# The opening of a two-layer hybrid diffusion step: smaller first parts, x requested first

## The chip, the cores and the metric

One Trainium2 chip, one of its cores. The metric is the device time of one execution in microseconds (us), median of the runs. One launch computes both layers.

## The reference, cut to what matters

Every layer normalizes x, modulates it with vectors that come from a conditioning vector, and multiplies it by the input projection. The change concerns this beginning in layer 0; attention, output projection and feed-forward follow and are left as they are.

```python
D_MODEL = 2048; SEQ = DEC_SEQ = 128; DEPTH = 2; IN_WIDTH = 4608
def modulation(cond, w_mod, b_mod):            # w_mod: 2048 x 12288
    m = jax.nn.silu(cond) @ w_mod + b_mod
    return jnp.split(m[..., None, :], N_MOD, axis=-1)
...
sm, cm, gm, sf, cf, gf = modulation(c_ctx, mod_w[l], mod_b[l])
h = rms_norm(xp, norm_mix_pre[l]) * (1 + cm) + sm
q_a, k_a, v_a, q_b, k_b, v_b, u_c, v_c = split_projection(h, w_in[l])   # h @ w_in
```

There are two token streams (context and latent, 128 tokens each, called s = 0 and 1), each with its own conditioning vector. All is float32.

## The kernel before, in words

**Products.** A weight piece is 256 rows by 512 columns, 512 KB. SyncE (SP) loads it into a ring of four places (`raw`); ScalarE rounds it into `whi` (fp32r), VectorE writes the rest `raw - whi` into `wlo`, each in rings of four places too. TensorE then does 12 matmuls per piece (`products`, line 956): 2 row blocks of 128, 2 streams, and the three products lo*hi, hi*lo, hi*hi. The activations stand as `xt_hi` and `xt_lo`, transposed, in 16 tiles of 128 rows, k = 0 to 15. `split(q+4)` runs four pieces ahead of TensorE (`LEAD`) and needs the place that piece q gives back when TensorE is done with it (`place_free`, line 529). SP loads raw piece q after `lo_ready` shows piece q-4 split.

**Modulation.** The vectors shift and scale of layer 0 are the first two of six. Each chunk m of 512 columns takes 8 pieces of 512 KB (2 tiles of 128 rows by 512 columns each); `MOD_INIT` = 8 chunks give the two vectors, `start_chunk` puts them in the order 0, 4, 1, 5, 2, 6, 3, 7, so that one chunk of shift and the same chunk of scale come together. A chunk's products go to `bank_M`, ScalarE copies the bank to `mrow` (`row`, line 1297), TensorE turns it by 4 transposes into `bank_T` (`vector_turn`, line 1037), VectorE reduces it into `modt` (`mod_cols`, line 1591). A burst is half a chunk, 4 pieces, put between two pieces of the input projection. Chunks 0 and 1 come ahead of everything; 21 further bursts are at `START_BURSTS`.

**The first unit of layer 0** (`start()`, on TensorE line 966, ScalarE line 1396, VectorE line 1726) is cut into four quarters of `QUARTER` = 18 pieces, q = 0 to 71. Quarter n works with x tiles 4n to 4n+3 only, over all 9 column chunks, two pieces for each chunk. Such a pair of pieces is a visit: it uses banks A0, A1 or B0, B1 in turn, and at its end VectorE reads the banks into z (`read_part`, line 1751; copy in quarter 0, line 1759, and addition later, line 1757). TensorE may begin visit e when visit e-2 is read (`free`). The four engines follow programs written out by hand; VectorE's order for each q is: `split(q+4)`, then the read at a visit's end, then a mod chunk's reduction three pieces after its burst, then the preparation of the next quarter at r = 13 (`part(n+1)`: the vectors, the scaling of two x blocks, the low halves). At r = 12 TensorE has turned the x blocks (`turn_x`).

**The order of the loads.** SP asks for chunk 0 (8 pieces), q = 0, chunk 1 (8), q = 1 to 3, chunk 2 (8), then q = 4, 5, ... with further mod pieces behind loads g+3 and g+4 of a burst at g (`START_FETCH`). Chunks 0 and 1 and half of chunk 2 stand in places of their own; later mod pieces use a ring of four (`mraw`) and wait until the piece four before is used (`mod_room`). GpSimd (POOL) loads 12 constants and then x, one megabyte for each stream. ScalarE does silu of the conditioning, then squares x (8 operations), from which VectorE and GpSimd make the norm. Loads for attention start on POOL when piece `ATT_PIECE` - 1 = 61 of the unit is done.

Of the kernel before, what the change touches and what calls it, by code (L numbers as in the profile page):

```python
# [48 lines left out]
MOD_INIT = 2 * ND  # L49
MOD_WIN = W_INC // 2  # L50
# [101 lines left out]
def ring_piece(m=None, j=0, v=None, i=0):  # L152

    if v is None:
# [15 lines left out]
PE_AT = {ring_piece(m, j): m * UNIT + j for m, j in pe_pieces()}  # L170


N_AT_ONCE = 3 * UNIT


def own_place(q):

    return RING <= q < 2 * UNIT or 2 * UNIT + RING <= q < N_AT_ONCE


def ring_turn(q):

    return q if q < RING else q - (2 * UNIT - RING) if q < 2 * UNIT + RING else q - 2 * UNIT


def ring_before(q):

    n = ring_turn(q) - RING
    return n if n < RING else n + (2 * UNIT - RING) if n < 2 * RING else n + 2 * UNIT
# [32 lines left out]
def mod_tail_of(m):  # L222

    return m if m < MOD_INIT else vector_tail(vector_of(m))


def vector_tail(v):

    return MOD_INIT + v - 2
# [4 lines left out]

def start_piece(q):

    n, r = divmod(q, QUARTER)
    return n, r // 2, 2 * n + r % 2


START_BURSTS = [QUARTER * n + r for n, rs in enumerate(((1, 4, 7, 10, 14), (1, 4, 7, 10, 13, 16), (1, 4, 7, 10, 13, 16), (1, 4, 7, 13)))
                for r in rs]
START_MOD = {g: (2 + i // 2, range(4 * (i % 2), 4 * (i % 2) + 4)) for i, g in enumerate(START_BURSTS)}
START_ENDS = {g: m for g, (m, js) in START_MOD.items() if js[0] and (m < MOD_INIT or m == MOD_INIT + ND - 1)}
ATT_PIECE = QUARTER * 3 + 8
START_FETCH = {g + 3 + h: (m, js[2 * h:2 * h + 2]) for g, (m, js) in START_MOD.items() if m > 2 for h in range(2)}
# [12 lines left out]
class Plan:  # L259
# [3 lines left out]
    def __init__(self):  # L263
# [10 lines left out]
        for l in range(DEPTH):  # L274
# [4 lines left out]
            self.takes(["A0", "A1"], (W_INC + 1) // 2 if l else ND * W_INC // 2)  # L279
            self.takes(["B0", "B1"], W_INC // 2 if l else ND * W_INC // 2)  # L280
# [76 lines left out]
def build_program(nc, a):  # L357
# [8 lines left out]
    with ExitStack() as ctx:  # L366
# [98 lines left out]
        first_landed = [sem(f"first_landed_{i}") for i in range(2 * UNIT)]  # L465
# [84 lines left out]
        def mod_done(l, v):  # L550

            gv = l * 6 + v
            return (gv + 1) * ND if gv < 2 else vector_tail(gv) + 1
# [8 lines left out]
        def mod_place(q):  # L562

            if not own_place(q):
                return mraw[:, q % RING]
            i = q - RING
            if i >= 2 * UNIT:
                hi = spare[:].rearrange("p k t -> p (k t)")
                lo = gate_ffn[:].rearrange("p s d -> p (s d)")
                t = (hi, lo)[i % 2][:, (4 + 4 * (i // 2 % 2)) * 2 * P:][:, 0:KB * CH]  # L570
                return t.rearrange("p (t n) -> p t n", t=KB)
            if i >= 10:
                return (hid, sil)[i - 10][:]
            t = z[:, i // 4, i % 4 * KB * CH + 4 * P:][:, 0:KB * CH] if i < 8 else qkt[:, 8 * (i - 8):8 * (i - 7), :].rearrange(
                "p h c -> p (h c)")
            return t.rearrange("p (t n) -> p t n", t=KB)
# [10 lines left out]
        def mraw_ready(engine, q):  # L587

            if own_place(q):
                engine.wait_ge(first_landed[q - RING if q < 2 * UNIT else q - 2 * RING], 16)  # L590
# [3 lines left out]
        def xt_count(l, which):  # L594


            return 8 + 9 * (2 * l + which)
# [14 lines left out]
        def vec_count(l, which):  # L612

            return 2 * l + which + ND
# [10 lines left out]
        def _(sp):  # L625
            def mod_room(q):

                if q < RING or own_place(q):
# [41 lines left out]
            def mod_chunk(m, l, js=range(UNIT), col=None):  # L670

                for j in js:
                    q = ring_piece(m, j)
                    if m < MOD_INIT:
                        src = a["mod_w"][l, j * KB * P:(j + 1) * KB * P, col * CH:(col + 1) * CH]
                        mod_room(q)
                        sp.dma_start(mod_place(q), src.rearrange("(t p) n -> p t n", p=P)).then_inc(
                            first_landed[q - RING if q < 2 * UNIT else q - 2 * RING] if own_place(q)
                            else mraw_landed[q % RING], 16)
# [28 lines left out]
            for m in range(2):  # L708
                mod_chunk(m, 0, range(UNIT), start_chunk(m))
# [1337 lines left out]
```

## Time and profile before

| | |
|---|---|
| median of 3 runs | 2320.89 us (2319.48 to 2322.94) |
| profiled execution, its time | 2317.93 us |
| its span, first to last instruction | 2316.2 us |
| busy: PE / DVE / ACT | 97% / 70% / 43% of the span |
| granted TensorE clock, mean | 0.996 |
| chain that ended last, share of PE | 87% |
| moved by DMA | 610 MB, 263 GB/s over the span |

PE is TensorE's matmuls, PEld its weight loads, DVE VectorE, ACT ScalarE, SPq the queue of SyncE. Times in rows are us from the span's start unless they say ns; "x24" is the number of instructions merged in a row; what stands in brackets is idle time before it and what ended that. The end of a matmul is modelled, so a short stall between two can be missing.

### The profile page before, as it was taken

What the parts mean: (1) busy time and instruction counts of PE and PEld (TensorE: products, weight loads), DVE (VectorE), ACT (ScalarE), POOL (GpSimd) and SP (SyncE); (2) the same over time, 40 slices, a digit from 0 to 9 for tenths busy, and PEclk for the clock granted to TensorE, in tenths of its full rate; (3) what the DMA queues carried; (4) which work ended last, traced back from release to release, by engine and by line L of the source; (5) the groups of instructions that cost most, each with busy time, mean ns of one, the idle gap of its engine ahead of it and who ended that gap; (6) DMA issues with size and microseconds to landing.
All of it is one profiled execution on the core that took longest, in us unless ns stands there. A gap on an engine that the chain in (4) does not pass through costs nothing.

```text
span 2316.2 us, 27842 instructions
## 1 busy us (share of the span) xinstructions
PE 2247.0 (97%) x10614; PEld 1778.0 (77%) x10614; DVE 1622.3 (70%) x1734; ACT 984.9 (43%) x1277; POOL 66.5 (3%) x97
## 2 busy tenths in 40 slices
PE   5999989999999999999999999999999999999998
PEld 3766666678888888888877886787888888888886
DVE  3555473488988989889887996557888544554555
ACT  3333253464444444334446344346444444434443
POOL 1000120000000000000000101000000000000000
PEclk9999999999999999999999999999999999999999
DMA  9899989868878878888866998766887666666664
GB/s 364 323 334 341 337 317 330 300 220 289 282 271 292 289 265 283 295 279 290 307 209 225 312 315 283 271 204 207 270 263 263 185 196 185 190 189 193 191 225 146
DMA packets 269365, 609.91 MB, mean 263 GB/s; under 512 B 19100, under 2 KB 19280, under 8 KB 267824
## 3 DMA queue, kind: packets, MB, share of 16 engines
q1 hardware_dynamic: 264832, 589.37, 75.4%
q0 software_dynamic: 4400, 18.75, 2.3%
q8 instruction: 85, 1.39, 0.2%
q14 instruction: 48, 0.39, 0.0%
HBM read 603.79 MB, written 5.45 MB: 263 GB/s over the span
## 4 chain that ended last, share of the span: by engine, by line
PE 87%; DVE 4%; DMA 4%; ACT 3%; issue 1%; POOL 1%; SPq 1%; POOLq 0%; DVEq 0%; ACTq 0%
PE bank_A L961 41%; PE bank_B L961 39%; DMA mraw<-in_mod_w 3%; PE bank_X L1049 2%; PE bank_M L1025 2%; DVE wlo L1564 1%; PE bank_M L1009 1%; ACT junk L1285 1%; ACT whi L1271 1%; DMA x<-in_x_sample 0%; DVE x L1674 0%; ACT prob L1436 0%; PE bank_M L950 0%; DVE xt_lo L1615 0%; PE bank_T L1042 0%
## 5 line engine op out<-in xcount | busy, mean ns | idle before, releaser
L1564 DVE TENSOR_TENSOR wlo<-raw,whi 128x1024 fp32r<-128x1024 f32 x724 | 880.6, 1223 | 587.3 <-ACT whi L1271 586.4
L1271 ACT CAST whi<-raw 128x1024 fp32r<-128x1024 f32 x724 | 759.5, 1051 | 1162.6 <-PE bank_A L961 575.5
L961 PE MATMUL bank_B<-whi,xt_lo 128*128 128x512 f32 x1104 | 433.3, 392 | 0.0
L961 PE MATMUL bank_A<-whi,xt_lo 128*128 128x512 f32 x1088 | 428.9, 394 | 3.7 <-DVE xt_lo L1615 3.7
L961 PE MATMUL bank_B<-wlo,xt_hi 128*128 128x512 f32 x1104 | 430.0, 389 | 0.0
L961 PE MATMUL bank_B<-whi,xt_hi 128*128 128x512 f32 x1104 | 429.8, 389 | 0.0
L961 PE MATMUL bank_A<-wlo,xt_hi 128*128 128x512 f32 x1088 | 425.0, 391 | 0.0
L961 PE MATMUL bank_A<-whi,xt_hi 128*128 128x512 f32 x1088 | 424.7, 390 | 0.0
L1585 DVE SCALAR_TENSOR_TENSOR acc<-mraw,cond,acc 128x1024 f32<-128x1024 f32 x300 | 371.2, 1279 | 0.0
L961 PEld LDWEIGHTS bank_A<-whi,xt_lo 128*128 128x128 f32 x1088 | 205.0, 188 | 65.1 <-issue 23.2
L961 PEld LDWEIGHTS bank_B<-whi,xt_lo 128*128 128x128 f32 x1104 | 207.2, 188 | 53.8 <-issue 11.7
L961 PEld LDWEIGHTS bank_B<-whi,xt_hi 128*128 128x128 f32 x1104 | 207.2, 188 | 43.7
L961 PEld LDWEIGHTS bank_B<-wlo,xt_hi 128*128 128x128 f32 x1104 | 207.3, 188 | 42.1
L961 PEld LDWEIGHTS bank_A<-whi,xt_hi 128*128 128x128 f32 x1088 | 204.9, 188 | 43.6
L961 PEld LDWEIGHTS bank_A<-wlo,xt_hi 128*128 128x128 f32 x1088 | 204.9, 188 | 41.6
L961 PE MATMUL bank_A<-whi,ht_lo 128*128 128x512 f32 x352 | 138.3, 393 | 0.7 <-DVE wlo L1564 0.7
L961 PE MATMUL bank_B<-whi,ht_lo 128*128 128x512 f32 x352 | 137.6, 391 | 0.2 <-DVE wlo L1564 0.2
L961 PE MATMUL bank_A<-whi,ht_hi 128*128 128x512 f32 x352 | 137.1, 389 | 0.0
L961 PE MATMUL bank_B<-wlo,ht_hi 128*128 128x512 f32 x352 | 137.0, 389 | 0.0
L961 PE MATMUL bank_A<-wlo,ht_hi 128*128 128x512 f32 x352 | 137.0, 389 | 0.0
L961 PE MATMUL bank_B<-whi,ht_hi 128*128 128x512 f32 x352 | 137.0, 389 | 0.0
L961 PEld LDWEIGHTS bank_A<-whi,ht_lo 128*128 128x128 f32 x352 | 66.1, 188 | 16.7 <-issue 2.3
(242 smaller groups left out, 1567.7 us busy)
## 6 DMA issues: line engine op xcount, KB each, us to landing
mraw<-in_mod_w SPq DMA_DIRECT2D x352, 512.0 KB, 6.0
raw<-in_w_gate SPq DMA_DIRECT2D x176, 512.0 KB, 4.4
raw<-in_w_up SPq DMA_DIRECT2D x176, 512.0 KB, 4.4
raw<-in_w_down SPq DMA_DIRECT2D x176, 512.0 KB, 5.0
raw<-in_w_in SPq DMA_DIRECT2D x144, 512.0 KB, 5.4
raw<-in_w_out SPq DMA_DIRECT2D x64, 512.0 KB, 5.8
z<-in_mod_w SPq DMA_DIRECT2D x12, 512.0 KB, 11.5
spare<-in_mod_w SPq DMA_DIRECT2D x8, 512.0 KB, 9.5
```

The lines of the kernel that those rows point to most:

```text
L961: mm = pe.matmul(bank[f"{pair}{s}"][:], xs[:, k, t], w[:, kb, :], start=(k == first and n == 0), stop=(k == (nk - 1 if last is None else l ...
L1009: mm = pe.matmul(bank["M"][g:g + 32, :], cond[:, 2 * k:2 * k + 32], w[:, kb, :], start=(k < 4), stop=(k >= KD - 4))
L1025: mm = pe.matmul(bank["M"][32 * c:32 * c + 32, :], cond[:, 2 * k:2 * k + 32], w[:, c % 2, :], start=(k == 0), stop=(k == KD - 1))
L1049: mm = pe.transpose(bank[b][:, n * P:(n + 1) * P], t, ident[:])
L1271: act.copy(weights(u * UNIT + ph)[0], raw[:, ph % RING]).then_inc(hi_ready, 1)
L1285: act.activation(junk[:], src, ACT.Square, accum_out=dst).then_inc(sq_ready, 1)
L1564: dve.tensor_tensor(lo, raw[:, ph % RING], hi.bitcast(F32), ALU.subtract).then_inc(lo_ready, 1)
L1585: ins = dve.scalar_tensor_tensor(out=to, in0=w, scalar=c, in1=to, op0=ALU.mult, op1=ALU.add)
```

## The change

- `HALVED` = 2: chunks 0 and 1 are worked as halves of 256 columns. A piece is now 4 tiles of 128 rows by 256 columns (still 512 KB, contiguous rows of 1 KB in place of 2 KB), and four pieces make a complete half. Only the first half of each comes ahead of the projection. The second halves are bursts after q = 1 and q = 4. Their copies, transposes and reductions are done for each half (2 transposes in place of 4).
- The first quarter's x tiles come as two parts of two: `PARTS` is {0,1}, {2,3}, {4..7}, {8..11}, {12..15}. Pieces q = 0 to 8 go over the 9 column chunks with tiles 0 and 1, q = 9 to 17 with tiles 2 and 3. So in the first quarter each piece is a visit of its own, with its own bank pair and its own read into z.
- The scaling and the low halves for tiles 2 and 3 come at q = 7, those for tiles 4 to 7 at q = 16 (before: r = 13).
- Bursts are now after q = 6, 9, 11, 13 in the first quarter (before: 1, 4, 7, 10, 14); quarters two and three keep r = 1, 4, 7, 10, 13, 16; quarter four has 1, 4, 7, 9, 13 (before: 1, 4, 7, 13). In all 21 as before, and the two halves besides.
- SP asks for x first, then first half of chunk 0 (4 pieces), q = 0, first half of chunk 1 (4), q = 1, 2 pieces, q = 2, 2 pieces, q = 3, 4 pieces (the second halves), then q = 4, 5, ...; chunk 2 isn't loaded ahead any more. ScalarE squares x ahead of silu.
- `ATT_PIECE` - 1 goes from piece 61 to piece 63.

```diff
+PARTS = [range(0, 2), range(2, 4), range(4, 8), range(8, 12), range(12, 16)]
+VISITS = 2 * W_INC + (ND - 1) * W_INC
 def start_piece(q):
     n, r = divmod(q, QUARTER)
-    return n, r // 2, 2 * n + r % 2
+    return (r // W_INC, r % W_INC, r // W_INC) if n == 0 else (n + 1, r // 2, 2 * n + r % 2)
...
+    return q if q < QUARTER else QUARTER + (q - QUARTER) // 2
...
+START_HALVES = {1: 0, 4: 1}
+START_BURSTS = [QUARTER * n + r for n, rs in enumerate(((6, 9, 11, 13), (1, 4, 7, 10, 13, 16), (1, 4, 7, 10, 13, 16), (1, 4, 7, 9, 13)))
...
+START_TURNS = {QUARTER * n + 12: n + 1 for n in range(ND - 1)}
+START_SCALES = {7: 1, 16: 2, QUARTER + 13: 3, 2 * QUARTER + 13: 4}
+ATT_PIECE = QUARTER * 3 + 10
...
-            for m in range(2):
-                mod_chunk(m, 0, range(UNIT), start_chunk(m))
-                for q in range(1, LEAD) if m else range(1):
-                    start_load(q)
-            mod_chunk(2, 0, range(UNIT), start_chunk(2))
+            for s in range(2):
+                sp.dma_start(x[:, s, :], xin[s]).then_inc(x_loaded, 16)
+            mod_chunk(0, 0, range(0, 4), start_chunk(0))
+            start_load(0)
+            mod_chunk(1, 0, range(0, 4), start_chunk(1))
+            for q, (m, js) in enumerate(((0, range(4, 6)), (0, range(6, 8)), (1, range(4, 8)))):
+                start_load(q + 1)
+                mod_chunk(m, 0, js, start_chunk(m))
...
             def start():
-                for m in range(2):
-                    mod(m)
-                    mod_tail(m)
+                mod(0, range(0, 4))
+                start_tail(0)
                 turn_x(0, 0, 0)
                 turn_x(0, 0, 1)
+                mod(1, range(0, 4))
+                start_tail(1)
...
+            def halved_piece(m, j):
+
+                q = ring_piece(m, j)
+                w = mod_place(q) if q in OWN else mraw[:, q % RING].rearrange("p t (h n) -> p (t h) n", n=CH // 2)
+                for t in range(4):
+                    k = 4 * (j % 4) + t
+                    mm = pe.matmul(bank["M"][32 * t:32 * t + 32, 0:CH // 2], cond[:, 2 * k:2 * k + 32], w[:, t, :],
+                                   start=(k < 4), stop=(k >= KD - 4))
+                mm.then_inc(mod_used, 1)
...
                 for q in range(ND * QUARTER):
-                    n, c, _ = start_piece(q)
-                    r = q % QUARTER
+                    p, c, _ = start_piece(q)
                     split(0, q + LEAD)
-                    if r % 2:
-                        read_part(n, c, q)
+                    if visit_ends(q):
+                        read_part(p, c, q)
                     if q - 3 in START_ENDS:
-                        m = START_ENDS[q - 3]
-                        mod_cols(m, start_chunk(m))
-                    if n + 1 < ND and r == 13:
-                        part(n + 1)
+                        start_cols(START_ENDS[q - 3])
+                    if q in START_SCALES:
+                        part(START_SCALES[q])
```

## Rows read from the trace of the kernel before

**Rows 1.** The page, the span in 40 slices of 57.9 us.

```profile
GB/s 364 323 334 341 337 317 330 300 220 289 282 271 292 289 265 283 295 279 290 307 209 225 312 315 283 271 204 207 270 263 263 185 196 185 190 189 193 191 225 146
```

**Rows 2.** Stretches: length, busy us (instructions) of five engines, TensorE clock, DMA.

```profile
20.70:38.20 17.50, 8.17 (x49) 3.26 (x49) 6.59 (x19) 9.87 (x23) 0.73 (x1) 0.90 1.05 408
...
38.19:45.45 7.26, 7.26 (x24) 5.53 (x25) 4.99 (x7) 1.77 (x2) 1.18 (x2) 0.76 1.05 405
...
45.30:283.80 238.50, 233.66 (x1182) 161.18 (x1181) 133.56 (x170) 81.91 (x93) 8.77 (x13) 1.00 0.93 333
...
80.00:98.00 18.00, 18.00 (x94) 13.60 (x93) 11.00 (x19) 8.13 (x12) 0.55 (x1) 1.00 0.68 234
```

**Rows 3.** Waits of TensorE, 45 to 285 us: total, times, longest.

```profile
PE bank_M L1025 <- DMA mraw<-in_mod_w: 3.9, 3, 2.6
```

**Rows 4.** Timeline up to the first product: start, us, engine, operation, idle before.

```profile
14.75 0.23 ACT L1467 ACTIVATE silu_c<-vcols 128x32 f32<-128x32 f32 x1 [12.73 <-DVE vcols L1905]
...
15.25 3.58 PE L1009 MATMUL bank_M<-mraw,cond 128*32 128x512 f32 x16 [1.26 <-DVE cond L1907]
...
19.13 0.63 ACT L1285 ACTIVATE junk<-x 128x512 f32<-128x512 f32 x1 [4.14 <-DMA x<-in_x_sample]
...
25.03 0.57 ACT L1300 COPY mrow<-bank_M 128x512 f32<-128x512 f32 x1
...
32.33 0.59 ACT L1300 COPY mrow<-bank_M 128x512 f32<-128x512 f32 x1 [5.79 <-PE bank_M L1009]
...
38.19 0.47 PE L961 MATMUL bank_A<-whi,xt_lo 128*128 128x512 f32 x1 [3.69 <-DVE xt_lo L1615]
```

**Rows 5.** Timeline of ScalarE: piece q = 4 is rounded.

```profile
47.73 1.05 ACT L1271 CAST whi<-raw 128x1024 fp32r<-128x1024 f32 x1 [7.76 <-DMA raw<-in_w_in]
```

**Rows 6.** The chain that ended last, in order of time: pieces and a burst.

```profile
38.19 7.33 PE bank_A L961 x24
...
47.37 5.71 PE bank_B L961 x24
53.08 2.72 PE bank_A L961 x12
55.80 1.85 PE bank_M L1009 x16
```

**Rows 7.** Timeline of VectorE: split of piece 6, read of the second visit.

```profile
54.26 1.23 DVE L1564 TENSOR_TENSOR wlo<-raw,whi 128x1024 fp32r<-128x1024 f32 x1 [0.62 <-ACT whi L1271]
55.40 1.28 DVE L1759 TENSOR_SCALAR z<-bank_B 128x512 f32<-128x512 f32 x2
56.97 1.23 DVE L1564 TENSOR_TENSOR wlo<-raw,whi 128x1024 fp32r<-128x1024 f32 x1 [0.29 <-ACT whi L1271]
```

**Rows 8.** Timeline of VectorE: the preparation of the second quarter.

```profile
92.01 0.18 DVE L1599 TENSOR_REDUCE modt<-bank_T 128x8 f32<-128x32 f32 x1
...
92.71 1.37 DVE L1645 TENSOR_SCALAR xtmp<-bank_X,scal,shift 128x128 f32<-128x128 f32 x4
94.77 1.29 DVE L1615 TENSOR_TENSOR xt_lo<-xtmp,xt_hi 128x512 fp32r<-128x512 f32 x2 [0.69 <-ACT xt_hi L1289]
```

**Rows 9.** Timeline of TensorE: first matmul of the second quarter (q = 18).

```profile
101.34 0.39 PE L961 MATMUL bank_B<-whi,xt_lo 128*128 128x512 f32 x1
```

**Rows 10.** The chain again: mod pieces' landings, and a burst behind one.

```profile
101.48 7.85 DMA mraw<-in_mod_w
...
270.18 11.50 DMA mraw<-in_mod_w
281.81 2.00 PE bank_M L1025 x8
...
285.09 6.97 DMA raw<-in_w_out
```

**Rows 11.** Timeline of GpSimd: the first load for attention.

```profile
259.67 0.87 POOL L784 DMA_DIRECT2D prob<-in_cache_a_k  x1 [162.51 <-PE bank_A L961]
```

**Rows 12.** DMA queues, 262 to 274 us: packets, MB, share of 16 engines.

```profile
q0 software_dynamic: 772, 2.20, 67.7%
```

More of the change, by code:

```diff
@@ L49 @@
 MOD_INIT = 2 * ND
+HALVED = 2
 MOD_WIN = W_INC // 2
@@ L152, in ring_piece @@
 def ring_piece(m=None, j=0, v=None, i=0):
+    if v is None and m < HALVED:
+        return UNIT * (j // 4) + 4 * m + j % 4
     if v is None:
@@ L168, in vector_of @@
     return 0 if m < MOD_INIT else MOD_PE[(m - MOD_INIT) // ND]
[L170 to L178, printed above, removed]
+PE_AT = {ring_piece(m, j): ring_piece(m, j) if m < HALVED else m * UNIT + j for m, j in pe_pieces()}
+OWN = [*range(0, 12), *range(16, 20)]
 def ring_turn(q):
-    return q if q < RING else q - (2 * UNIT - RING) if q < 2 * UNIT + RING else q - 2 * UNIT
+    return q - (12 if q < 16 else 16)
 def ring_before(q):
-    n = ring_turn(q) - RING
-    return n if n < RING else n + (2 * UNIT - RING) if n < 2 * RING else n + 2 * UNIT
+    return q - RING if q >= 24 else q - 2 * RING
 BANKS = ["A0", "A1", "B0", "B1", "M", "X0", "X1", "T"]
@@ L464, in build_program @@
         mraw_landed = [sem(f"mraw_landed_{i}") for i in range(RING)]
-        first_landed = [sem(f"first_landed_{i}") for i in range(2 * UNIT)]
+        first_landed = [sem(f"first_landed_{i}") for i in range(len(OWN))]
+        part_scaled = [sem(f"part_scaled_{s}") for s in range(2)]
         apart_landed = [sem(f"apart_landed_{i}") for i in range(4)]
@@ L594, in xt_count @@
         def xt_count(l, which):
-            return 8 + 9 * (2 * l + which)
+            return 10 + 9 * (2 * l + which)
         def z_complete(engine, l):
@@ L612, in vec_count @@
         def vec_count(l, which):
-            return 2 * l + which + ND
+            return 2 * l + which + len(PARTS)
         N_CONST = 12
@@ L796, in _ @@
             load(edge[:], a["c_edge"], const_loaded)
-            for s in range(2):
-                load(x[:, s, :], xin[s], x_loaded)
             def power(src, dst, s_in, n_in, s_out):
@@ L1040, in vector_turn @@
                 free("T", i)
-                for t in range(4):
+                for t in range(2 if i < 2 * HALVED else 4):
                     mm = pe.transpose(bank["T"][:, t * P:(t + 1) * P], mrow[:, t * P:(t + 1) * P], ident[:])
@@ L1299, in row, with start_row, pre_part @@
                     act.wait_ge(filled["T"], i)
-                act.copy(mrow[:], bank["M"][:]).then_inc(mrow_ready, 1)
+                c = slice(0, CH // 2 if i < 2 * HALVED else CH)
+                act.copy(mrow[:, c], bank["M"][:, c]).then_inc(mrow_ready, 1)
+            def start_row(i):
+                act.wait_ge(mod_used, 4 * (i + 1) if i < 2 * HALVED else
+                            (i - HALVED) * UNIT + UNIT if i - HALVED < MOD_INIT else (MOD_INIT + ND) * UNIT)
+                row(i)
+            def pre_part(p):
+                fill_of(*plan.at[(0, "pre_uses", 0)][1])
+                bk, n = plan.at[(0, "pre_uses", 0)][1]
+                for k in PARTS[p]:
+                    ins = act.activation(xtmp[:, 0, 1, k, :], bank[bk][:, k * P:(k + 1) * P], ACT.Identity,
+                                         scale=scal[:, k, 1:2], bias=shift[:, k, 1:2])
+                ins.then_inc(freed[bk] if p else part_scaled[1], 1)
+                for s in range(2):
+                    bk, n = plan.at[(0, "pre_uses", 0)][s]
+                    if p:
+                        act.wait_ge(freed[bk], n + 2)
+                    else:
+                        act.wait_ge(part_scaled[s], 1)
+                    ks = slice(PARTS[p][0], PARTS[p][-1] + 1)
+                    high(xt_hi[:, ks, s * P:(s + 1) * P], xtmp[:, 0, s, ks])
             def pre_scale(l, which, i):
```

158 lines of the change are left out of this document (94 added, 64 removed).

## The prediction

> **What bounds the kernel now.** I read the slices of the whole span first [rows 1]: DMA moves 300 to 364 GB/s in the first eight slices (463 us) and 146 to 225 in the last eight, so memory can only matter early. The stretches come next [rows 2]. From 20.7 to 38.2 us DMA runs full, 408 GB/s, while TensorE is busy for 8.17 of 17.5 us: there the data decide. From 45.3 to 283.8 us TensorE is busy for 233.66 of 238.5 us, at the full clock, with DMA at 333 GB/s: there TensorE's own program decides, and its waits for data are three, 3.9 us in all [rows 3]. From 80 to 98 us DMA falls to 234 GB/s while TensorE is full: the rings hold the loads back, not memory. So after the opening, whatever makes TensorE idle is lost for good, and a microsecond won at the first product counts only if the products behind it come as early.
>
> The timeline to the first product [rows 4] shows what the change attacks. The constants give silu at 14.75, chunk 0's matmuls go from 15.25, but x lands only at 19.13, its eight squares hold ScalarE to 25.0, and the copy of chunk 0 stands behind them at 25.03. Chunk 1 is complete at 32.33, and the first product starts at 38.19.
>
> **The first product.** Landings follow from bytes, since DMA is full. Piece q = 4 is rounded at 47.73, right after a wait for its data [rows 5]. Ahead of its landing stand 29 pieces with it (8+1+8+3+8+1) of 0.524 MB, x (2.10) and the constants (0.46): 17.8 MB. After the change 21 pieces stand there (4+1+4+1+2+1+2+1+4+1), 13.6 MB in all: 4.19 MB less, at 408 GB/s 10.3 us less. So q = 4 can be rounded at 37.4. The first half of chunk 1 is complete after 7.3 MB, 15.4 us before that, at 22.0. x is first and lands near 10; squares to 16, silu behind them, half of chunk 0 for 3.6 us at the clock of the first burst [rows 4], its copy and turn and the eight turns of x for some 2 us: 22. Then the half of chunk 1, 1.85 [rows 6] to 3.6 us, and what is 5.9 us now (32.33 to 38.19) less 0.9 for x's turns, done already, and about 1.4 for work on two tiles in place of four: 3.6. First product at 27.5 to 29.2, some 9 us sooner.
>
> **The third piece.** Here the gain is cut. Each of the first 18 pieces is now a visit with banks of its own, and TensorE may start visit q only when VectorE has read visit q-2. VectorE's order is split(q+4), then the read of q. The read of q = 0 stands behind the split of q = 4, so behind its landing: 37.4, rounding 1.05, split 1.23 with the read's 1.28 [rows 7] give 40.95. TensorE by then has done q = 0 and 1 and the second half of chunk 0 (7.3 us warm, 9.2 with the slow stretch of 7.33 for 24 matmuls in place of 5.44 [rows 6]): ready at 36 to 38, idle for 3 to 5 us. Now q = 2 starts at 47.37 [rows 6], so it comes 6.4 us sooner. But less mod work is done by then: 20 of 21 bursts are still to come at that point now, and 22 of 23 after the change. Two bursts at 1.85: 3.7 us of the 6.4 are owed.
>
> **The first quarter as a recurrence.** A piece is 2.72 us, a burst 1.85 [rows 6]. From the end of a piece to the end of its read: 53.08 to 56.68, 3.60 us (wait, rounding, split, read) [rows 6, 7]; with the wake-up 3.65. Now that stands beside two further pieces (5.44) and is hidden; after the change one piece (2.72) covers it, and 0.93 us show wherever no burst, turn (0.87) or tail (0.27) stands between. Worked from q = 2 at 40.95: q = 4 waits 0.65 for the read of q = 2. q = 7 ends at 62.2. Behind its read VectorE now prepares tiles 2 and 3. The same for four tiles takes 92.01 to 96.06, 4.05 us [rows 8]; two tiles, by halving the four- and two-instruction groups but not the 0.7 us ahead of them, 2.5. So q = 9 starts at 62.2+3.6+2.5+0.3 = 68.6, where q = 8 was done at 64.9: 3.7 us idle. The burst after 11 comes two pieces behind the burst after 9, whose ring places it needs: its four pieces and a raw piece land about 8 us after the places come free (a mod piece takes 7.85 us to land in such company [rows 10]), so its last piece waits about 1.0. q = 16 waits 0.6. q = 16 ends at 99.0; its read, the 4.05 of the full preparation and 0.35 give 107.0 for q = 18, where q = 17 was done at 101.7: 5.3 us idle. Before, this preparation stood at r = 13, three pieces earlier in the order and thus hidden. Stalls in all 0.65+3.7+1.0+0.6+5.3 = 11.3.
>
> Now q = 18 starts at 101.34 [rows 9]; after, at 107.0. It is 5.7 us late, and one burst more (17 against 16) is still to come: 7.5.
>
> **The rest.** Quarters two and three have the bursts where they were and cost nothing new; their cover is 5.4 us for each read, as now. In the last quarter the burst after 63 is two pieces behind that after 61, again 1.0: 8.5. [...] After the gap before 38.19 the clock is 0.76 in the next 7.26 us [rows 2], 1.9 us lost; after the 2.63 us for the burst at 281.81, eight matmuls take 2.00 in place of 1.07 [rows 10], 0.9 lost. Three new gaps at 0 to 1.9 each: 0 to 5, taken as 1.0, like the nearer row: 3.0. Given back: the burst after 67 now waits 2.6 us [rows 3] for data that take 11.5 us to land beside attention's loads, asked for from 259.67 [rows 10, 11]; these come two pieces later now. It may save 0 to 3.5 (stall and clock); I take 1.5, as output-projection pieces (6.97 us to land [rows 10]) meet those loads instead. Sum 8.5+3.0-1.5 = 10.0 us. Against the profiled execution, 2317.9 (1.7 more than its span), that is 2327.9. The median shown is 3.0 above that execution; on it the forecast is 2331.
>
> **Rows of 1 KB.** No row shows the halved pieces' load (a row of 256 columns is 1 KB in place of 2). The nearest end is that it moves like the 2 KB rows, cost 0. The far end is the software queue with its 256 to 512 byte rows: 2.20 MB in 67.7% of 12 us [rows 12] is 271 GB/s of full engines against 389 (408 at share 1.05). Sixteen such pieces, 8.4 MB, would take 9.4 us more, and q = 2 would come that much later. [...] I take 0, nearer in kind (same queue, double length), and half the far end, 4.7, for the range. The Trainium skill (DMA: Bandwidth & Descriptors, Specifications) gives 512 bytes as the least for line rate, by which this would cost nothing; the trace has no hardware-queue load with rows under 2 KB to test it.
>
> The Trainium skill (TensorE: Matmul & The Clock Gate, HAM oscillation) speaks against the change's gaps: idle stretches between matmul groups drop the clock, and the work behind them runs slow. The slow matmuls behind 38.19 and 281.81 agree; by it the sum would sit at the upper end, 10.0+2.0.
>
> **The rivals.** (1) The first product is what counts, and the rest keeps its pace. For it: TensorE is busy for 98% behind 45 us, and 9 us are won at the front. Then 9.7 less 3.7 for the two bursts moved behind, with 1 to 3 from the burst after 67: about -8, 2313. It needs VectorE's reads not to hold TensorE: that q = 2 not wait for q = 4's landing, which the order split-before-read contradicts. (2) The mechanism is mine but the stalls are short: preparation of two blocks overlaps more than I think, the clock holds, the burst at 67 doesn't wait. 6.4-3.7 = 2.7 lead against 5 to 7 of stalls and no clock loss: 0 to +4, 2321 to 2325. (3) Slow rows of 1 KB, or the clock low through much of the first quarter: +13 to +19, 2334 to 2340. (4) The start is limited by memory all through, so that TensorE's extra idle time only replaces waits for data: against it, DMA at 234 GB/s from 80 to 98 and 3.9 us of data waits in 238; it would give 2320.9. It goes into (2).
>
> **How the numbers follow.** Forecast (+5 to +13, 2326 to 2334) 0.60; (1) 0.10; (2) with (4) 0.18, a little of it below; (3) 0.12. The predicted time is 2331. The range for 8 in 10 runs from 2320 (case 2's lower end, leaving out case 1) to 2338 (case 3's middle and above). A measurement of this kernel can tell 0.2%, 4.6 us, from no change: slower than 2325.5 is the forecast, case 3 and a bit of case 2, 0.72; faster than 2316.3 is case 1, 0.10; within, 0.18.
>
> **What would show it.** In the profile of the changed kernel: the first product between 27 and 30 us; an idle gap of 3 to 5 us before the third piece, released by a VectorE read near 41 that follows a wait of ScalarE for raw data; TensorE waits on the read of the banks of about 0.9 us in the first quarter; gaps of 3 to 4 us before q = 9 and some 5 us before q = 18, each ending on an xt_lo operation; q = 18 near 107 to 111. I'm wrong if q = 2 starts before 36, if q = 18 starts before 101, or if the first quarter shows no waits for VectorE.

## The result and the profile after

The changed kernel takes 2342.60 us (median of 4 runs, 2338.84 to 2343.79), the kernel before 2321.91 (4 runs, 2319.48 to 2323.30): ratio 1.0086, 95% interval 1.0071 to 1.0100, so 20.7 us slower. The profiled execution took 2341.53, its span is 2339.7. The forecast was 2331, in a range up to 2338: the sign was right, the size half of what came, and the time lies outside the range.

The page of the kernel after, DMA rate in 40 slices. The last eight are nearly what they were [rows 1]; the first two are lower, 334 and 269 against 364 and 323.

```profile
GB/s 334 269 310 328 357 323 312 298 207 300 288 265 290 291 262 293 286 283 289 289 243 201 309 333 259 300 192 212 254 278 261 196 192 188 189 189 195 192 220 149
```

**The first product comes 10.9 us sooner.** Timelines of ScalarE and TensorE of the kernel after, up to the first product (start, us, engine, line, operation, idle before):

```profile
8.59 0.63 ACT L1331 ACTIVATE junk<-x 128x512 f32<-128x512 f32 x1 [6.56 <-DMA x<-in_x_sample]
...
14.60 1.28 ACT L1542 ACT_TABLE_LOAD   x1
15.90 0.23 ACT L1542 ACTIVATE silu_c<-vcols 128x32 f32<-128x32 f32 x1
...
16.40 3.40 PE L1055 MATMUL bank_M<-z,cond 128*32 128x256 f32 x32 [2.26 <-DVE cond L1991]
...
21.54 1.93 PE L1055 MATMUL bank_M<-z,cond 128*32 128x256 f32 x32
...
27.34 0.77 PE L989 MATMUL bank_A<-whi,xt_lo 128*128 128x512 f32 x1 [2.93 <-DVE xt_lo L1691]
```

x's squares begin at 8.59, not 19.13; half of chunk 0 goes at 16.40, half of chunk 1 at 21.54, and the first product starts at 27.34, where it was 38.19 [rows 4]. A second table load of 1.28 us has come in ahead of silu, which now stands behind the squares.

**At the third piece half of that is gone.** The chain of waits of the kernel after, in order of time (start, us, what):

```profile
29.34 9.29 DMA raw<-in_w_in
...
38.65 1.05 ACT whi L1317
...
40.87 0.69 DVE z L1843
...
42.25 5.08 PE bank_A L989 x12
```

The landing of raw piece q = 4 (38.6) releases the rounding, the rounding the split, the split lets VectorE come to the read of q = 0 at 40.87, and that read lets q = 2 start at 42.25. TensorE had been idle for 4.62 us, and its next twelve matmuls took 4.91 us instead of 2.72 (counted here and below from start to start; the chain's 5.08 goes to the end of the last one). In the kernel before q = 2 started at 47.37 [rows 6]: the lead is 5.1 us.

**At q = 18 the lead is a lag.** Waits of TensorE of the kernel after, 27 to 118 us (total, times, longest):

```profile
PE bank_A L989 <- DVE xt_lo L1691: 8.0, 2, 5.1
PE bank_A L989 <- DVE z L1843: 5.3, 2, 4.6
PE bank_B L989 <- DVE xt_lo L1691: 3.7, 1, 3.7
...
PE bank_M L1045 <- DMA mraw<-in_mod_w: 0.4, 1, 0.4
```

The 8.0 are 2.93 before the first product and 5.09 before q = 18; the 5.3 are 4.62 before q = 2 and 0.72 before q = 4; the 3.7 stand before q = 9. These three are waits for VectorE, where the kernel before had none from its first product to 285 us. VectorE of the kernel after, timeline of the preparation ahead of q = 18:

```profile
109.78 1.28 DVE L1841 TENSOR_TENSOR z<-z,bank_A 128x512 f32<-128x512 f32 x2
110.97 0.18 DVE L1675 TENSOR_REDUCE modt<-bank_T 128x8 f32<-128x32 f32 x1
...
113.72 1.29 DVE L1691 TENSOR_TENSOR xt_lo<-xtmp,xt_hi 128x512 fp32r<-128x512 f32 x2 [0.68 <-ACT xt_hi L1335]
```

It takes 4.04 us, as before [rows 8], but it now follows the read of q = 16, and q = 18 starts right behind it, at 115.28. Before, q = 18 started at 101.34 [rows 9]: 13.9 us late. (Leads and lags are against one trace of the kernel before, and that trace is a quick one: in the trace of experiment 3, of a kernel with the same opening, the first product starts at 39.60, q = 2 at 48.61 and q = 18 at 103.34.)

Stretches of the kernel after (length, busy us and instructions of TensorE, its weight loads, VectorE, ScalarE, GpSimd, then TensorE's granted clock, DMA share, GB/s):

```profile
42.25:115.28 73.03, 62.63 (x309) 42.93 (x309) 43.98 (x69) 22.07 (x30) 0.53 (x1) 0.94 0.78 274
...
115.28:304.65 189.37, 180.72 (x909) 122.96 (x909) 99.96 (x126) 59.72 (x67) 8.20 (x12) 0.98 0.91 325
...
42.20:47.30 5.10, 5.05 (x13) 4.03 (x14) 2.29 (x3) 0.00 (x0) 0.00 (x0) 0.56 0.81 256
...
72.90:77.50 4.60, 4.55 (x16) 3.19 (x20) 2.42 (x3) 0.25 (x1) 0.53 (x1) 0.63 0.39 127
...
115.20:122.50 7.30, 7.22 (x28) 5.61 (x32) 3.63 (x4) 1.05 (x1) 0.00 (x0) 0.78 0.27 74
```

From q = 2 to q = 18 the kernel after takes 73.0 us, the one before took 54.0. Of the 73.0, 10.4 are idle. Behind each of the three gaps the granted clock is low, 0.56, 0.63 and 0.78 of 2.4 GHz: the twelve matmuls of q = 2 take 4.91 us, those of q = 9 4.46, where 2.72 is the full clock's, and the 24 of q = 18 and 19 take 7.2 where they took 5.6 in the kernel before. That makes 2.2, 1.7 and 1.6, in all 5.5 us.

Two bursts are slow without a long wait in the list. TensorE's timeline of the burst after q = 11:

```profile
85.37 1.93 PE L1045 MATMUL bank_M<-mraw,cond 128*32 128x512 f32 x12
87.67 1.05 PE L1045 MATMUL bank_M<-mraw,cond 128*32 128x512 f32 x4 [0.37 <-DMA mraw<-in_mod_w]
```

It takes 3.28 us, where a burst whose data are there takes 1.85, and the burst after q = 13 takes 2.54. Their weight loads wait for the mod pieces one by one, 2.8 us in four waits between 60 and 115 us.

**The last quarter takes 4.5 us more in two waits.** Waits of TensorE of the kernel after, 118 to 310 us, and the chain of waits there:

```profile
PE bank_M L1071 <- DMA mraw<-in_mod_w: 8.1, 5, 5.9
```

```profile
275.81 7.24 DMA mraw<-in_mod_w
...
283.18 1.13 PE bank_M L1071 x8
...
284.64 17.93 DMA mraw<-in_mod_w
...
302.71 1.94 PE bank_M L1071 x8
304.64 6.38 PE bank_B L989 x24
```

The burst after 63 waits 1.22 us for a landing of 7.24. The one after 67 waits 5.87 for a landing of 17.93 us, where it waited 2.6 for one of 11.50 [rows 3, 10]. The first of attention's twelve loads goes out at 281.55, 3.1 us ahead of that landing's start; before, it was 259.67 [rows 11]. GpSimd's timeline of the kernel after:

```profile
281.55 0.87 POOL L815 DMA_DIRECT2D prob<-in_cache_a_k  x1 [207.78 <-PE bank_A L989]
```

The piece behind that burst starts at 304.57, before at 283.68, a lag of 20.9 us. It stays to attention's first turn of z, 320.16 against 299.31. The spans differ by 23.5, so some 2.6 us come later: TensorE waits 1.6 us for a mod piece near 459 us, and some 1.1 us are added between 1120 and 1510 us, far from the change, where experiment 9's trace loses over 3 us against the same trace of the kernel before. The medians differ by 20.7.

### The profile page after: what moved, and what is told of

Its sections match the earlier page's. It is cut to its first block, busy times and chain, and to the rows that moved or that the text cites. A ratio compares the mean times of both kernels' runs of the same rounds, so it can differ in the third digit from the quotient of the medians.

```text
span 2339.7 us, 28083 instructions
## 1 busy us (share of the span) xinstructions
PE 2255.2 (96%) x10678; PEld 1786.5 (76%) x10678; DVE 1634.3 (70%) x1759; ACT 986.4 (42%) x1282; POOL 65.5 (3%) x95
## 4 chain that ended last, share of the span: by engine, by line
PE 85%; DMA 5%; DVE 5%; ACT 3%; issue 2%; SPq 1%; POOL 0%; POOLq 0%; DVEq 0%; ACTq 0%
PE bank_A L989 40%; PE bank_B L989 38%; DMA mraw<-in_mod_w 4%; PE bank_X L1095 2%; PE bank_M L1071 2%; DVE wlo L1635 1%; PE bank_M L1045 1%; ACT junk L1331 1%; ACT whi L1317 1%; DVE acc L1656 0%; DVE x L1750 0%; SPq L668 0%; ACT prob L1507 0%; DMA raw<-in_w_in 0%; PE bank_M L978 0%
## 5 line engine op out<-in xcount | busy, mean ns | idle before, releaser
L989 PE MATMUL bank_A<-whi,xt_lo 128*128 128x512 f32 x1092 | 433.3, 397 | 13.9 <-DVE xt_lo L1691 8.0
```

What stands on the lines that cost most here:

```text
L989: mm = pe.matmul(bank[f"{pair}{s}"][:], xs[:, k, t], w[:, kb, :], start=(k == first and n == 0), stop=(k == (nk - 1 if last is None else l ...
```

## The experiments

All times are medians; the ratio is to the kernel before on the same chip, with its 95% interval, which is about 3 us to either side; of a difference between two of the kernels below it is about 4. Differences of less than that are carried by the traces, not by the times.

**1. Reads ahead of splits.** The kernel after, in whose first quarter VectorE reads the banks of piece q before it splits q+4:

```diff
                     p, c, _ = start_piece(q)
+                    if q < QUARTER:
+                        read_part(p, c, q)
                     split(0, q + LEAD)
-                    if visit_ends(q):
+                    if q >= QUARTER and visit_ends(q):
                         read_part(p, c, q)
```

> The changed kernel with one thing altered: in the first quarter VectorE reads a piece's banks ahead of the split of the piece four further on. Theory R (what holds the first quarter is the read queued behind the split, 3.6 us after a piece's end against 2.72 of cover): the 4.6 us idle before the third piece goes, the third piece starts near 37.7 in place of 42.25, the waits of 0.5 to 0.9 for reads go, the slow matmuls behind the gap at 42.25 (2.2 us) go in part; the gaps before q = 9 (3.7) and q = 18 (5.1) get shorter by some 1 us at most. But q = 4 can't start before its own split, about 41 to 42, so the win at q = 4 is only what remains: start near 43.2 against 51.02. In all 6 to 9 us less than the changed kernel's 2342.6: 2334 to 2337. Rival M (memory, not the order of reads, holds the first pieces): the idle time moves to the wait for the raw pieces q = 4 and 5 and at most 2 us are won: 2340 to 2343.

Measured: 2334.98 us, ratio 1.0053 (1.0039 to 1.0066), 7.6 less than the kernel after. Waits of TensorE of this kernel, 27 to 110 us:

```profile
PE bank_A L989 <- DVE xt_lo L1691: 6.9, 2, 4.0
PE bank_B L989 <- DVE xt_lo L1691: 2.6, 1, 2.6
PE bank_B L989 <- DVE z L1845: 2.2, 1, 2.2
```

q = 2 starts at 37.26 without a gap. The wait has moved to q = 3, for the read of q = 1, which stands behind the split of q = 4, and is 2.2 us in place of 4.6. The gaps before q = 9 and q = 18 fall from 3.7 to 2.6 and from 5.1 to 4.0, and q = 18 starts at 106.47. The burst after 67 still waits 5.4. So the order split-before-read is a cause, of some 8 us; it is not the whole.

**2. Keeping the clock up.** The kernel after, with matmuls into the free bank T ahead of q = 2, 9 and 18, whose results nobody reads:

```diff
+WARM = {2: (2, 8), 9: (4, 6), 18: (6, 8)}
...
                     pair = "AB"[e % 2]
+                    if q in WARM:
+                        free("T", WARM[q][0])
+                        for _ in range(WARM[q][1]):
+                            pe.matmul(bank["T"][:], ident[:], vcols[:], start=True, stop=True)
```

> The changed kernel with idle TensorE filled in its three gaps: 8, 6 and 8 extra 128x512 matmuls into bank T ahead of q = 2, 9 and 18, whose results nobody reads. The order of the real work is untouched. Theory C (a good part of the excess is the low clock behind the gaps): q = 2 takes 2.7 in place of 4.9 us, q = 9 2.7 in place of 4.5, the two pieces from q = 18 5.8 in place of 7.2: together 5 to 5.5 us less, 2337. Rival: the low clock's loss is absorbed by later waits (the reads, the bursts' data), and the time stays within 2 us of 2342.6.

Measured: 2346.66 us, ratio 1.0110 (1.0096 to 1.0123). The dummies took 0.8 us each and overran every gap (37.36 to 43.93, 70.22 to 75.07, 112.70 to 119.28), so the time decides nothing. The trace showed one thing: q = 2 then took 3.15 us in place of 4.91, q = 9 3.26 in place of 4.46. I repeated it with 5, 3 and 3 of them:

```diff
-WARM = {2: (2, 8), 9: (4, 6), 18: (6, 8)}
+WARM = {2: (2, 5), 9: (4, 3), 18: (6, 3)}
```

> The changed kernel with its three gaps filled by fewer extra matmuls: 5, 3 and 3 of 128x512 into bank T, 4.5, 2.7 and 2.7 us, which fit the gaps of 4.6, 3.7 and 5.1 us (the earlier 8, 6 and 8 overran them: the first batch took from 37.36 to 43.93, 1.7 us too long). Theory C (the low clock behind the gaps costs 2.2, 1.7 and 1.4 us): q = 2 in 2.8 to 3.2 us in place of 4.9, q = 9 in 3.2 in place of 4.5, q = 18 earlier by 3 to 4 us in all: 2338 to 2340. Rival: q = 2's gain is swallowed by the waits for reads behind it, and the total gains under 2 us.

Measured: 2337.42 us, ratio 1.0062 (1.0050 to 1.0074), 5.2 less than the kernel after. TensorE's timeline of this kernel:

```profile
37.16 4.56 PE L1011 MATMUL bank_T<-vcols,ident 128*128 128x512 f32 x10
42.46 0.47 PE L990 MATMUL bank_A<-whi,xt_lo 128*128 128x512 f32 x1 [0.74 <-DVE z L1848]
```

q = 2 starts at 42.46, no sooner than before the edit, but q = 3 follows 2.8 us later, at 45.26; q = 9 takes 2.9, and q = 18 and 19 5.7. The gaps are as long as they were, only filled, and the pieces behind them take 5.1 us less in all: the low clock cost about 5 us, beside the idle time itself. The rival holds in small: the burst after 11, reached sooner, takes 4.38 us in place of 3.28, and q = 20 starts 4.4 us sooner (119.85 against 124.26). The Trainium skill (TensorE: Matmul & The Clock Gate, HAM oscillation) says that idle stretches between groups of matmuls throttle what follows; these runs agree, with 1.6 to 2.2 us behind a gap of 3.7 to 5.1.

**3. Attention's loads eight pieces sooner**, in the kernel after and in the kernel before (there six):

```diff
-ATT_PIECE = QUARTER * 3 + 10
+ATT_PIECE = QUARTER * 3 + 2
```

> The changed kernel with only the start of attention's 12 loads moved, from the end of piece 63 to the end of piece 55, 8 pieces sooner. Theory L (the loads' 2.2 MB come at the very moment at which the burst after 67 fetches its last pieces, and hold these up): the wait of 5.87 us in that burst falls below 1, the slow matmuls behind it go, 5 to 8 us less in all: 2335 to 2338. Rival: the wait moves to the bursts after 58, 61 or 63, which then meet the loads, and no more than 2 us are won.

> The kernel before with only attention's loads moved, from the end of piece 61 to the end of piece 55. The same theory L: the wait of 2.63 us in the burst after 67 and its slow matmuls (0.9 and about 0.5) go: 3 to 4 us less than 2321.9, 2318. Rival: the bursts after 58 and 61 pay as much, and the time stays within 1 us.

Measured: 2346.97 us, ratio 1.0108 (1.0095 to 1.0121), 4.4 more than the kernel after; and 2330.42, ratio 1.0038 (1.0026 to 1.0050), 8.5 more than the kernel before. My theory that the collision could be had away by an earlier start fell in both. The rivals had the place right (another burst pays); that both kernels would be slower for it, neither theory nor rival had. The chains of waits, first of the kernel after with this edit, then of the kernel before with it:

```profile
255.84 15.37 DMA mraw<-in_mod_w
...
271.35 1.93 PE bank_M L1071 x8
```

```profile
243.47 15.95 DMA mraw<-in_mod_w
...
259.55 1.94 PE bank_M L1025 x8
```

The burst after 67 no longer waits, but the one after 58 does, 6.8 and 7.1 us: the loads delay the mod pieces in flight beside them to 15 us and more, and a burst that stands three pieces (8.2 us) behind the last one has less cover than one that stands six behind it.

**4. The cover given back.** The kernel after, with the fifth burst of the last quarter moved to the first, and the loads where they were before:

```diff
-START_BURSTS = [QUARTER * n + r for n, rs in enumerate(((6, 9, 11, 13), (1, 4, 7, 10, 13, 16), (1, 4, 7, 10, 13, 16), (1, 4, 7, 9, 13)))
+START_BURSTS = [QUARTER * n + r for n, rs in enumerate(((6, 9, 11, 13, 16), (1, 4, 7, 10, 13, 16), (1, 4, 7, 10, 13, 16), (1, 4, 7, 13)))
...
-ATT_PIECE = QUARTER * 3 + 10
+ATT_PIECE = QUARTER * 3 + 8
```

> The changed kernel with the burst after piece 63 taken back: last quarter 1, 4, 7, 13 as in the kernel before, the burst put after q = 16 of the first quarter, attention's loads again behind piece 61. Theory G (attention's loads cost what isn't covered by the pieces between one burst and the next; six pieces cover more than four): the wait of 5.87 us in the burst after 67 goes back to about 2.6, the wait of 1.2 in the burst after 63 goes, 3 to 5 us less in all: 2338 to 2340. Rival (the burst at 16 takes as much in the first quarter): within 1.5 us of 2342.6.

Measured: 2338.84 us, ratio 1.0072 (1.0057 to 1.0087), 3.8 less than the kernel after. The burst after 67 waits 2.4 us, for a landing of 10.34. The rival is refuted: the burst put after 16 falls into the gap before q = 18, which shrinks from 5.1 to 3.0, and q = 18 starts at 114.54, not later. Over all runs whose loads start right behind a burst, the next burst waits 6.8 to 7.1 us when it stands three pieces on, 5.4 to 6.0 with four, 2.3 to 3.4 with six. This run moves both the burst and the start of the loads, so what either does alone is not separated.

**5. Bursts and preparations sooner.** The kernel after, with the bursts of the first quarter one or two pieces sooner and its two preparations one and two:

```diff
-START_HALVES = {1: 0, 4: 1}
-START_BURSTS = [QUARTER * n + r for n, rs in enumerate(((6, 9, 11, 13), (1, 4, 7, 10, 13, 16), (1, 4, 7, 10, 13, 16), (1, 4, 7, 9, 13)))
+START_HALVES = {1: 0, 3: 1}
+START_BURSTS = [QUARTER * n + r for n, rs in enumerate(((5, 7, 9, 11), (1, 4, 7, 10, 13, 16), (1, 4, 7, 10, 13, 16), (1, 4, 7, 9, 13)))
...
-START_SCALES = {7: 1, 16: 2, QUARTER + 13: 3, 2 * QUARTER + 13: 4}
+START_SCALES = {6: 1, 14: 2, QUARTER + 13: 3, 2 * QUARTER + 13: 4}
```

> The changed kernel with the first quarter's mod bursts after q = 1, 3, 5, 7, 9, 11 in place of 1, 4, 6, 9, 11, 13, and the two preparations at q = 6 and q = 14 in place of 7 and 16. Theory P (the gaps of 3.7 and 5.1 us before q = 9 and q = 18, with slow matmuls of 1.7 and 1.4 behind them, come from preparations too close to their use): both gaps shrink below 1, some 9 to 11 us go, less 1 to 2 for bursts only two pieces apart: 2333 to 2336. Rival: bursts two pieces apart wait for their data 2 to 3 us each and the halves' second part isn't there at q = 3, so at most 4 us are won: 2338 or more.

Measured: 2340.00 us, ratio 1.0077 (1.0062 to 1.0092), only 2.6 less than the kernel after, not 7 to 10. Waits of TensorE of this kernel, 27 to 110 us:

```profile
PE bank_A L989 <- DVE z L1843: 4.7, 1, 4.7
PE bank_B L989 <- DVE z L1841: 3.6, 1, 3.6
...
PE bank_B L989 <- DVE z L1843: 1.6, 1, 1.6
PE bank_T L1088 <- DVE modt L1675: 1.1, 1, 1.1
```

The waits for xt_lo before q = 9 and q = 18 are gone as they should be. In their place stand waits of 1.6 and 3.6 us, before q = 9 and q = 17, for reads that queue behind the preparation and the split next to it: 5.2 of the 8.8. q = 17, behind the longer, takes 5.26 us at the low clock. The rival had the total right and half of the cause: the bursts after 9 and 11, two pieces apart, take 2.93 and 3.99 us in place of 1.85, and the turn of the second half waits 1.1 for bank T, whose last reduction queues behind a split and a read, but the second half's own data at q = 3 were there. (The trace is of the slowest of the four executions, 2344.48 us.) A preparation in a run of one-piece visits holds TensorE at its own place as well as at the place of its use.

**6. Everything mended at once.** Reads first, bursts (3 for the second half; 5, 7, 9, 11, 15) and preparations (6, 14) sooner, the last quarter as before, and raw pieces 4 and 5 asked for ahead of the second half of chunk 1 (the edit, cut to what experiments 1, 4 and 5 don't show):

```diff
+START_BURSTS = [QUARTER * n + r for n, rs in enumerate(((5, 7, 9, 11, 15), (1, 4, 7, 10, 13, 16), (1, 4, 7, 10, 13, 16), (1, 4, 7, 13)))
...
-            for q, (m, js) in enumerate(((0, range(4, 6)), (0, range(6, 8)), (1, range(4, 8)))):
+            for q, (m, js) in enumerate(((0, range(4, 6)), (0, range(6, 8)))):
                 start_load(q + 1)
                 mod_chunk(m, 0, js, start_chunk(m))
+            for q in range(3, LEAD + 2):
+                start_load(q)
+            mod_chunk(1, 0, range(4, 8), start_chunk(1))
```

> The changed kernel with all remedies: reads ahead of splits in the first quarter, bursts after 1, 3, 5, 7, 9, 11, 15, preparations at q = 6 and 14, last quarter 1, 4, 7, 13 with attention's loads behind piece 61, and raw pieces 4 and 5 loaded ahead of chunk 1's second half. If the excess is the sum of the causes (reads 7.6, preparations 9 to 11, gap 3 to 5, and 2 for q = 4 sooner), it comes to 2342.6 less 22 to 25: 2318 to 2321, up to 4 us under the kernel before. If they overlap (one stall absorbs the next): 2324 to 2330.

Measured: 2319.57 us (10 runs), ratio 0.9991 (0.9978 to 1.0004): 23.0 us less than the kernel after, and not to be told from the kernel before. Waits of TensorE of this kernel, 27 to 110 us, and the stretch from its first product to q = 18:

```profile
PE bank_A L993 <- DVE xt_lo L1695: 2.9, 1, 2.9
PE bank_M L1049 <- DMA mraw<-in_mod_w: 2.3, 2, 1.6
```

```profile
27.30:100.50 73.20, 70.67 (x380) 48.26 (x381) 50.73 (x78) 25.47 (x34) 1.71 (x3) 0.96 0.94 349
```

Behind the first product there is no wait for VectorE left, and both waits are for memory: the burst after 9, the fifth in a row two pieces apart, takes 5.40 us in place of 1.85. But q = 18 starts at 100.50, only 0.8 us sooner than in the trace of the kernel before, although the first product came 10.8 sooner. Two bursts more stand in this stretch (3.7), 2.5 us are idle, and TensorE's busy time is 3.8 longer than the 63.15 us of the stretch before from its first product to q = 18, with the two bursts added: that uses up 10.0 of the 10.8.

**7. The same with the reads behind the splits again.** To test the first cause where the others are absent:

```diff
                     p, c, _ = start_piece(q)
-                    if q < QUARTER:
-                        read_part(p, c, q)
                     split(0, q + LEAD)
-                    if q >= QUARTER and visit_ends(q):
+                    if visit_ends(q):
                         read_part(p, c, q)
```

> The mended kernel (2319.6) with one remedy taken back: in the first quarter the split of piece q + 4 stands ahead of the read of piece q again. Theory V (visits of one piece leave VectorE no room: each read, and each preparation that stands before a read, shows on TensorE): the third piece waits 1 to 2 us for the read behind the split of q = 4, four or five reads show 0.5 to 0.9 each, the preparation at q = 14 shows 2 to 3 us at q = 17, with slow matmuls behind it: 6 to 10 us more, 2326 to 2330. Rival (the 7.6 us of the earlier run were mostly the wait for q = 4's data, which comes sooner here): at most 3 us more, under 2323.

Measured: 2325.38 us, ratio 1.0013 (1.0005 to 1.0022), 5.8 more than with the reads first, a little under the 6 to 10 expected and above the rival's at most 3. Waits of TensorE of this kernel, 27 to 110 us:

```profile
PE bank_B L993 <- DVE z L1845: 1.9, 1, 1.9
PE bank_B L993 <- DVE z L1847: 1.6, 1, 1.6
PE bank_T L1092 <- DVE modt L1679: 1.1, 1, 1.1
```

4.6 us of waits for VectorE come back, two of them behind the preparations (before q = 9 and q = 17) and one for bank T; q = 17 takes 1.7 us longer at the low clock. The third piece hardly waits (0.24), where 1 to 2 were expected. The order of read and split is worth 6 to 8 us in either surrounding.

**8. Attention's loads one by one**, behind pieces 50 to 66, on top of 6:

```diff
-                pool.wait_ge(w_used, (plan.at[(l, "win")][0] + 4) * UNIT if l else ATT_PIECE)
+                steps = iter([51, 53, 54, 56, 57, 59, 60, 62, 63, 64, 66, 67])
...
+                    if l == 0 and s is att_loaded:
+                        pool.wait_ge(w_used, next(steps))
```

> The mended kernel with attention's 12 loads of layer 0 asked for one after the other, behind pieces 50 to 66, in place of all behind piece 61. Theory L2 (together they hold up whichever burst fetches next; one by one they fit into what the DMA engines have free): the waits of 0.7 and 2.6 us for mod data in the last quarter shrink below 1 in sum, and slow matmuls with them: 2 to 4 us less, 2316 to 2318. Rival (DMA is full through the last quarter, 0.9 of it, and every byte is paid): the waits spread over more bursts and the time stays within 1.5 us of 2319.6.

Measured: 2322.82 us, ratio 1.0005 (0.9996 to 1.0013), 3.2 more than without it, which the intervals don't tell from none. The mod pieces' waits from 200 to 310 us are still 4.0 us (4.9 in experiment 6), in three parts, the longest 2.2, and the wait ahead of attention's first turn of z is 4.3 us, where it was 1.8. Spreading them gained nothing; both theory and rival, which had at most 1.5 us more, missed.

**9. x first and nothing else.** The kernel before, with x asked for first by SyncE and its squares ahead of silu:

```diff
+            for s in range(2):
+                sp.dma_start(x[:, s, :], xin[s]).then_inc(x_loaded, 16)
             for m in range(2):
...
-            for s in range(2):
-                load(x[:, s, :], xin[s], x_loaded)
```

> The kernel before with x alone asked for first, by SP, and squared ahead of silu. Theory B (chunk 1's landing sets the first product, and that hangs on the bytes asked for, not on their order): chunk 0's copy comes 5 us sooner, the first product stays within 1 us of 38.19, and so does the total: 2321 to 2323. Rival (x is what the start waits for): first product 3 to 5 us sooner, total 2317 to 2319.

Measured: 2322.12 us, ratio 0.9998 (0.9988 to 1.0008): nothing. The first product starts at 39.30, in the range of the kernel before (38.19, and 39.60 in experiment 3's trace of it). Chunk 0's copy is done at 22.6, but chunk 1 arrives piece by piece, and only its last piece decides. So x asked for first isn't enough; the gain at the first product needs the halves (the halves without x first were not run).

The two first products of the kernel before differ with what DMA moved. Stretch of experiment 3's trace of it, against 408 GB/s in [rows 2]:

```profile
20.70:38.20 17.50, 9.44 (x54) 3.33 (x48) 5.36 (x17) 9.25 (x23) 0.72 (x1) 0.80 1.05 387
```

Experiment 9's trace has 387 in this stretch too.

**10. Rows of 2 KB.** The kernel after, with the halved pieces loaded as whole-width pieces of the same size:

```diff
-                        k, n, w = (j * KB * P, col * CH, CH) if m >= HALVED else (j % 4 * 4 * P, col * CH + j // 4 * (CH // 2), CH // 2)
+                        k, n, w = j * KB * P, col * CH, CH
```

> The changed kernel with chunk 0's and 1's pieces loaded as 2 tiles of 128 rows by 512 columns, rows of 2 KB, into the same places in the same order; the vectors of these chunks, and with them the output, are wrong, the work is the same. Theory N (rows of 1 KB cost next to nothing): q = 4 is rounded at 37.8 to 38.7 in place of 38.65, the total within 1.5 us of 2342.6. Rival (1 KB rows slow the opening): q = 4 rounded near 35 to 36, q = 2 as much sooner, 2338 to 2340.

Measured: 2341.55 us, ratio 1.0081 (1.0068 to 1.0094), 1.0 less than the kernel after. The stretch from 20 to 38 us, first of the kernel after, then of this one:

```profile
20.00:38.00 18.00, 13.91 (x100) 9.54 (x100) 8.64 (x17) 5.98 (x10) 1.38 (x2) 0.81 1.08 392
```

```profile
20.00:38.00 18.00, 14.05 (x104) 9.61 (x100) 8.63 (x17) 6.35 (x11) 1.36 (x2) 0.81 1.05 406
```

392 against 406 GB/s, and q = 4 is rounded at 38.65 against 37.75. Whether that 0.9 us is the price of the 1 KB rows is not shown. All ten traces with 1 KB rows have 392 or 393 in this stretch, on two chips. With 2 KB rows it is 406 here, 408 in [rows 2], but 387 in the two traces of experiments 3 and 9, both from the other chip: on this chip the 1 KB rows were 3.4% slower, on that one no slower. The Trainium skill (DMA: Bandwidth & Descriptors, Specifications) has everything from 512 bytes at line rate; these runs don't contradict it by more than 3.4%. The value taken, 0, was near, and the far end of 9.4 us is out.

## Why the prediction had the first quarter's mechanism right and the size wrong

**First product: right.** 27.34, 0.2 before the 27.5 to 29.2 forecast. The rival that counts this lead in full (2313) is refuted: 10.9 us of lead there were 5.1 at q = 2.

**Third piece: right, 1.3 us too early.** Forecast 40.95 after an idle stretch of 3 to 5; measured 42.25 after 4.62. q = 4 was rounded at 38.65, not 37.4: I let DMA move 408 GB/s, it moved 392, which on 13.6 MB is 1.4 us. Experiment 10 leaves open whether the rows of 1 KB made it so. (The far end took the software queue's rows as short; the trace shows their packets alone, 2.85 KB on average, 2.20 MB in 772 [rows 12].)

**Stalls of the recurrence: right.** In the forecast's order: q = 4 0.65, measured 0.72; q = 9 3.7, measured 3.68; the burst after 11 1.0, measured 0.4 idle; q = 16 0.6, measured 0.54; q = 18 5.3, measured 5.09. In all 11.3, measured 10.4. Experiments 1, 5 and 7 show the mechanism: the reads behind the splits, the preparations next to their use. The sign that missed is the last: q = 18 near 107 to 111, measured 115.28.

**The term missed in the first quarter: 3.1 us.** From q = 2 to q = 18 the recurrence gave 66.0 (40.95 to 107.0); 73.0 were measured, 3.9 of the difference being the clock, which the sum has apart. The other 3.1 are 4.0 of work that the recurrence had at nothing, less the 0.9 by which the stalls were shorter. Counted from start to start, the 4.0 are: 1.8 in the bursts after 11 and 13, whose pieces of data came one by one (3.28 and 2.54 us for 1.85, 0.37 of it counted above); 1.5 in fourteen pieces, which took up to 2.91 next to a burst or a turn where I used 2.72 throughout, as those of the kernel before do too; 0.7 in the turns of bank T.

**The clock: mis-sized, 3.0 for 5.5.** I took 1.0 for each of three gaps, after the row with 0.9 for a gap of 2.6. The new gaps were 3.7 to 5.1 long and cost 1.6 to 2.2, like the further row (1.9 behind the 3.7 us before 38.19 [rows 2, 4]). The gaps that I had forecast had that row's length, not the other's; experiment 2 gives back 5.1 behind them.

**The burst after 67: wrong in sign, the step that failed most.** I credited 1.5 us, because attention's loads come two pieces later. It waited 3.2 us longer instead. The credit looked only at when the loads start. The change had also taken the pieces between the two bursts at that place from six to four, by putting the burst after 63 in between, and the wait goes with that number in every run (experiments 3 and 4). I had priced that burst's own wait (1.0, measured 1.22), and not what it does to the next. This is the largest error, 4.7 us.

Summed at the end of the burst after 67, where the forecast had +10.0 and the trace has +20.9: 1.3 (q = 2) + 3.1 (first quarter) + 2.5 (clock) + 4.7 (burst after 67) + 0.4 (burst after 63, 3.28 us for 1.85 and the 1.0) = 12.0, against 10.9 to be explained. Against it stand 1.0 us that the kernel before lost in quarters two to four and this one didn't: its other bursts there ran 4.0 us over 1.85, here 3.5, and a turn waited 0.45 for `mrow`.

**As remedies**, each alone on the kernel after: reads first 7.6, the cover in the last quarter 3.8, preparations and bursts sooner 2.6, in all 14.0; experiment 6, which holds these three and the loads of q = 4 and 5 sooner, gave 23.0. The 9.0 beyond the sum are not split further. Part is that the parts act on one another (preparations sooner pays only where the reads don't queue behind them), part the slow matmuls that go with the gaps (5.2 by experiment 2). So no single figure is a cause's share. **Open** are the part of the early loads, which were not run alone, what the loads' start and the bursts' spacing do each by itself in the last quarter, and whether a version with the early first product can beat the kernel before: the best, experiment 6, has an interval that holds 1.

## What to carry to other kernels

A start made sooner is worth only what the next stage's order lets through: before splitting visits, write out the serving engine's queue and look at which landing each bank's read stands behind. Shorter visits take the cover from every read and preparation at once, so reads go ahead of work that waits for data, and preparations away from their use; every gap that stays is priced with the slow matmuls behind it, from a row with a gap of the same length. When a burst is moved, price the neighbours whose spacing it changes, above all where another queue's loads come in.

## What the runs showed of the hardware

- Attention's twelve loads by GpSimd's queue come with landings of 10.3 to 17.9 us for the mod pieces in flight beside them, where others took 7.2 to 7.9, in all places tried. Where the cover was longest, started together, they cost the next burst 2.3 to 3.4 us of waits; one by one they gained nothing.
- Square ahead of silu costs one more table load of 1.28 us at the start; silu ahead of the squares did with one.
- Twelve 128x512 matmuls took 2.72 us from start to start in a run of pieces, 2.81 to 2.95 next to a burst or a turn of another shape, in the kernel before and after.
- Behind idle gaps of 3.7 to 5.1 us the granted clock was low (0.56 to 0.78 over the next 4.6 to 7.3 us) and cost 1.6 to 2.2 us each; matmuls that nobody reads, put into the gaps, gave 5.1 us back over three.
- Full DMA engines moved 392 GB/s with rows of 1 KB on both chips tried; with rows of 2 KB 406 on one (experiment 10) and 387 on the other (experiments 3 and 9).
